# Second feed-forward of a two-block transformer: up products with the weight tile stationary and 256 token columns moving, in place of token tiles stationary, 512 weight columns moving and transposes

## The reference

```python
def squared_relu_mlp(h, w_up, w_down):
    return jnp.square(jax.nn.relu(h @ w_up)) @ w_down

# second block: D_MODEL = 2048, D_FF_2 = 8192
hm = modulate(rms_norm(x, norm_mlp_w[layer]), sh_m, sc_m)
x = x + g_m * squared_relu_mlp(hm, w_mlp_up[layer], w_mlp_down[layer])
return rms_norm(x, final_norm_w)
```

## Time and profile before

| | |
|---|---|
| device time, median of 3 runs | 2152.56 us (2151.63 to 2153.01) |
| profiled execution, span from first to last instruction | 3618.6 us |
| mean granted TensorE clock in the profiled execution | 0.555 |
| TensorE busy | 3602.4 us, 10171 matmuls |
| weight loads busy | 2135.9 us |
| VectorE busy | 1553.3 us |
| ScalarE busy | 1100.0 us |
| read from memory | 483 MB |

### The profile page before, as it was taken

One profiled execution on the slowest core, in us unless ns is written; L12 is line 12 of the kernel. 1 busy time (PEld: TensorE's weight loads), 2 busy tenths in 40 slices (PEclk: granted clock), 3 DMA queues, 4 the chain that ended last, 5 costly groups with the idle time before them and its releaser, 6 DMA issues.

```text
span 3618.6 us, 32275 instructions
## 1 busy us (share of the span) xinstructions
PE 3602.4 (100%) x10171; PEld 2135.9 (59%) x10171; DVE 1553.3 (43%) x1903; ACT 1100.0 (30%) x1467; POOL 129.4 (4%) x232
## 2 busy tenths in 40 slices
PE   9999999999999999999999999999999999999999
PEld 5556855555555555555555567565555555555555
DVE  5555455554555554444453332343333323333334
ACT  3223423333223332233353242232222222222222
POOL 1000000000000000000000000000000000000000
PEclk5555555555555555555555555555555555555555
DMA  7544064555555555544433311344434434433432
GB/s 232 174 147 140 18 198 141 174 162 164 167 175 163 162 166 164 168 145 150 137 105 112 111 53 48 115 134 136 120 118 133 128 117 134 134 112 127 133 104 66
DMA packets 279981, 487.04 MB, mean 135 GB/s; under 512 B 26252, under 2 KB 118740, under 8 KB 278560
## 3 DMA queue, kind: packets, MB, share of 16 engines
q1 hardware_dynamic: 249472, 371.42, 33.2%
q0 software_dynamic: 30192, 113.72, 10.2%
q10 hardware_dynamic: 176, 0.08, 0.0%
HBM read 483.00 MB, written 2.11 MB: 134 GB/s over the span
## 4 chain that ended last, share of the span: by engine, by line
PE 99%; DMA 0%; ACT 0%; POOL 0%; DVE 0%; issue 0%; ACTq 0%; DVEq 0%; POOLq 0%
PE G L1968 29%; PE G L1967 29%; PE G L1966 29%; PE T L2244 2%; PE T L2396 1%; PE T L2160 1%; PE T L2000 1%; PE G L2376 1%; PE G L2140 1%; PE T L2048 0%; PE G L2033 0%; PE G L2032 0%; PE G L2031 0%; PE T L2185 0%; PE T L2187 0%; PE G L2408 0%
## 5 line engine op out<-in xcount | busy, mean ns | idle before, releaser
L1122 DVE TENSOR_TENSOR w_lo<-raw,w_hi 128x1024 fp32r<-128x1024 f32 (+1 forms) x704 | 857.9, 1219 | 1725.4 <-ACT w_hi L593 1723.6
L593 ACT ACTIVATE w_hi<-raw 128x1024 fp32r<-128x1024 f32 (+1 forms) x704 | 741.6, 1054 | 2018.6 <-PE G L1968 2007.7
L1966 PE MATMUL G<-w_hi,h_hi 128*128 128x512 f32 (+1 forms) x1656 | 955.7, 577 | 1.5 <-DVE h_lo L1222 1.0
L1968 PE MATMUL G<-w_hi,h_lo 128*128 128x512 f32 (+1 forms) x1656 | 950.4, 574 | 0.0
L1967 PE MATMUL G<-w_lo,h_hi 128*128 128x512 f32 (+1 forms) x1656 | 947.7, 572 | 0.0
L1966 PE MATMUL G<-w_hi,a_hi 128*128 128x512 f32 x1120 | 650.8, 581 | 0.0
L1967 PE MATMUL G<-w_lo,a_hi 128*128 128x512 f32 x1120 | 645.3, 576 | 0.0
L1968 PE MATMUL G<-w_hi,a_lo 128*128 128x512 f32 x1120 | 645.1, 576 | 0.0
L1966 PEld LDWEIGHTS G<-w_hi,h_hi 128*128 128x128 f32 x1656 | 363.9, 220 | 263.6 <-issue 154.2
L1968 PEld LDWEIGHTS G<-w_hi,h_lo 128*128 128x128 f32 x1656 | 361.4, 218 | 267.7 <-issue 155.5
L1967 PEld LDWEIGHTS G<-w_lo,h_hi 128*128 128x128 f32 x1656 | 364.8, 220 | 259.1 <-issue 152.6
(11 more groups left out here) (289 smaller groups left out, 1425.3 us busy)
## 6 DMA issues: line engine op xcount, KB each, us to landing
ada_w<-in_w_ada POOLq DMA_DIRECT2D x192, 512.0 KB, 3.9
raw<-in_w_up SPq DMA_DIRECT2D x352, 256.0 KB, 2.9
raw<-in_w_mlp_up SPq DMA_DIRECT2D x256, 256.0 KB, 2.8
raw<-in_w_mlp_down SPq DMA_DIRECT2D x256, 256.0 KB, 3.1
raw<-in_w_in SPq DMA_DIRECT2D x224, 256.0 KB, 2.9
raw<-in_w_down SPq DMA_DIRECT2D x176, 256.0 KB, 3.2
raw<-in_w_out SPq DMA_DIRECT2D x128, 256.0 KB, 3.2
raw<-in_w_in SPq DMA_DIRECT2D x16, 136.0 KB, 2.6
```

The lines of the kernel that those rows point to most:

```text
L593: act.activation(w_hi[:, s % 4, :, 0:width], raw[:, s % 8, :, 0:width], ACT.Copy).then_inc(hi_ready, 1)
L1122: dve.tensor_tensor(w_lo[:, s % 4, :, 0:width], raw[:, s % 8, :, 0:width], w_hi[:, s % 4, :, 0:width].bitcast(F32), ALU.subtract).then_inc ...
L1966: pe.matmul(out, ah, wh, start=f, stop=False)
L1968: mm = pe.matmul(out, al, wh, start=False, stop=l)
```

## The change

Of the second feed-forward's up chunks, the 128x128 tile of weights becomes the stationary operand and the 256 tokens the moving one (`up_steps`): for each tile three matmuls of 256 columns into the same columns of a bank, 24 matmuls a step. The result then has the hidden index on partitions, and `turn_up` is no longer called. An up chunk fills half of each of the four banks of `G` (even chunks) or `T` (odd ones); down chunks 0 and 1 use `G`, 2 and 3 use `T`. ScalarE's ReLU (two instructions of 512 columns, now from four half banks) moves from the chunk's end into the body of the next one; the square moves to VectorE (from `u_buf`), the rounding into `a_hi` to ScalarE. Before the 27 transposes at the start TensorE waits for `e0` instead of `e0 - 2`, that is for the last output bank of the phase before. The first row sum of the last group comes after 6 steps of its down chunk instead of before them.

```diff
+    def up_set(c):
+        return T if c % 2 else G
+    def down_set(c):
+        return T if c >= 2 else G
...
-        def post2(u, du):
-            def square():
-                act.wait_ge(turned, u + 1 + du)
-                act.wait_ge(a_ready, u + du)
-                act.activation(conv[:], tt(0), ACT.Square).then_inc(up_read, 1)
-            return square, lambda: None
-        def group2(s, u, d, du, begun=False, last=False):
+        e0 = FIRST_EVAC["mlp2"]
+        def post2(s, e, u, c, d, de, du):
+            def relu():
+                act.wait_ge(step_done, s + 8 * c + 8 + d)
+                act.wait_ge(bank_evac, e + 2 * c + de)
+                act.wait_ge(up_read, u + c + du)
+                for part in range(2):
+                    act.activation(u_buf[:, part, :].rearrange("p (t n) -> p t n", n=TOK),
+                                   up_set(c)[:, 2 * part:2 * part + 2, 0:TOK], ACT.Relu).then_inc(bank_evac, 1)
+            def high_part():
+                act.wait_ge(up_read, u + c + 1 + du)
+                act.activation(a_hi[:, 4 * c:4 * c + 4, :], conv[:], ACT.Copy).then_inc(a_first, 1)
+            return relu, high_part
+        def group2(s, e, u, d=0, de=0, du=0, begun=False, last=False):
             for c in range(4):
                 if c == 0 and begun:
                     his(s + 8, 3)
                 else:
-                    body(s + 8 * c, d, post2(u + c - 1, du) if c else None)
-                up_evac(c, s + 8 * c + 8, d, ACT.Relu)
...
-        def post2(u, c, du):
-            def split():
-                dve.wait_ge(up_read, u + 1 + du)
-                dve.tensor_copy(a_hi[:, 4 * c:4 * c + 4, :], conv[:]).then_inc(a_first, 1)
-                dve.wait_ge(a_first, u + 1 + du)
+        def post2(e, u, c, de, du):
+            def square():
+                dve.wait_ge(bank_evac, e + 2 * c + 2 + de)
+                flat = u_buf[:].rearrange("p b (t n) -> p (b t) n", n=TOK)
+                dve.tensor_tensor(conv[:], flat, flat, ALU.mult).then_inc(up_read, 1)
+            def low_part():
+                dve.wait_ge(a_first, u + c + 1 + du)
                 dve.tensor_tensor(a_lo[:, 4 * c:4 * c + 4, :], conv[:], a_hi[:, 4 * c:4 * c + 4, :].bitcast(F32),
                                   ALU.subtract).then_inc(a_ready, 1)
-            return lambda: None, split
-        def group2(s, u, d, du, first=0, dk=0, dt=0, begun=False, last=False):
+            return square, low_part
...
+        def up_steps(s, k0, k1, banks, ready, d=0):
+            for k in range(k0, k1):
+                pe.wait_ge(hi_ready, s + k + 1 + d)
+                pe.wait_ge(lo_ready, s + k + 1 + d)
+                pe.wait_ge(*ready(k))
+                for j in range(STEPK):
+                    kt = STEPK * k + j
+                    for t in range(CK):
+                        wh, wl = (w[:, (s + k) % 4, j, P * t:P * t + P] for w in (w_hi, w_lo))
+                        pe.matmul(banks[:, t, 0:TOK], wh, h_hi[:, kt, :], start=kt == 0, stop=False)
+                        pe.matmul(banks[:, t, 0:TOK], wh, h_lo[:, kt, :], start=False, stop=False)
+                        mm = pe.matmul(banks[:, t, 0:TOK], wl, h_hi[:, kt, :], start=False, stop=kt == KT - 1)
+                mm.then_inc(step_done, 1)
+        def down_steps(s, k0, k1, c, ready, d=0):
+            for k in range(k0, k1):
+                step(s + k, c % 2, A, STEPK * k, k == 0, k == 7, ready(k), d, banks=down_set(c))
...
-        def group2(s, e, u, d=0, de=0, du=0, begun=2, last=False):
+        def group2(s, e, u, d=0, de=0, du=0, begun=0, last=False):
             def ready(k):
                 return a_ready, u + k // 2 + 1 + du
-            if begun == 2:
-                steps(s, 0, 2, 0, H, r, e - 2, d, de)
             for c in range(4):
-                steps(s + 8 * c, 2 if c else begun, 8, c % 2, H, r, d=d)
-                if c < 3:
-                    steps(s + 8 * c + 8, 0, 2, (c + 1) % 2, H, r, e + 2 * c, d, de)
+                if begun == 0 or c:
+                    pe.wait_ge(bank_evac, e + (-4, 0, 2, 4)[c] + de)
+                up_steps(s + 8 * c, 0 if c else begun, 8, up_set(c), r, d)
+            for c in range(4):
+                pe.wait_ge(bank_evac, e + (6, 6, 8, 8)[c] + de)
+                first = s + 32 + 8 * c
+                if last and c == 0:
+                    down_steps(first, 0, 6, c, ready)
+                    pe.wait_ge(bank_evac, e + 8)
+                    row_sum(0)
+                    down_steps(first, 6, 8, c, ready)
+                elif last and c == 1:
+                    down_steps(first, 0, 4, c, ready)
+                    row_sum(1)
+                    down_steps(first, 4, 8, c, ready)
+                elif last and c == 3:
+                    pe.wait_ge(row_added, 2)
+                    down_steps(first, 0, 4, c, ready)
+                    last_steps(first + 4, A[0], 8, ready, 4, down_set(c))
                 else:
-                    steps(s + 32, 0, 2, 0, A, ready, e + 6, d, de)
-                turn_up(u + c, e + 2 * c + 2, d, du, de)
-            for c in range(4):
-                if last and c == 0:
-                    row_sum(0)
-                if last and c == 1:
-                    steps(s + 40, 0, 4, 1, A, ready, e + 8, d, de)
-                    row_sum(1)
-                    steps(s + 40, 4, 8, 1, A, ready, d=d)
-                else:
-                    steps(s + 32 + 8 * c, 2 if c == 0 else 0, 4 if last and c == 3 else 8, c % 2, A, ready, e + 8 + 2 * (c - 1), d, de)
-            if last:
-                last_steps(s + 60, A[0], 8, ready, 4)
-        pe.wait_ge(bank_evac, e0 - 2)
+                    down_steps(first, 0, 8, c, ready, d)
+        pe.wait_ge(bank_evac, e0)
         keep_busy(27, 0)
-        begin("up2", y, s0, 0, r)
+        begin("up2", y, lambda k: up_steps(s0, k, k + 1, up_set(0), r))
         group2(s0, e0, u0, begun=3)
         with pe.Fori(0, GROUPS2 - 2) as g:
             group2(s0 + 64, e0 + 16, u0 + 4, g * 64, g * 16, g * 4)
```

More of the change, by code:

```diff
@@ L1429, in _, with weighed @@
         first_fold(3)
-        def weighed(c, b):
-            dve.tensor_tensor(y[:, b, c * N:c * N + N], G[:, 2 * (c % 2) + b, :], row[:, c * N:c * N + N],
+        def weighed(c, b, banks=G):
+            dve.tensor_tensor(y[:, b, c * N:c * N + N], banks[:, 2 * (c % 2) + b, :], row[:, c * N:c * N + N],
                               ALU.mult).then_inc(bank_evac, 1)
@@ L1923, in g_row @@
             dve.wait_ge(row_added, half + 1)
[L1925 removed]
+        s0, e0, u0 = 2 * FIRST_LOAD["mlp2"], FIRST_EVAC["mlp2"], UP0["mlp2"]
         dve.wait_ge(y_zero, 1)
[L1927 removed]
+        group2(s0, e0, u0, begun=True)
         with dve.Fori(0, GROUPS2 - 2) as g:
[L1929 to L1930 removed]
+            group2(s0 + 64, e0 + 16, u0 + 4, g * 64, g * 16, g * 4, 8, g * 8, g * 4)
+        group2(s0 + 64 * (GROUPS2 - 1), e0 + 16 * (GROUPS2 - 1), u0 + 4 * (GROUPS2 - 1), first=8 * (GROUPS2 - 1), last=True)
         partial_means("final")
@@ L1952, in _, with step @@
     def _(pe):
-        def step(s, parity, acts, kt, first, last, ready=None, d=0, width=N):
+        def step(s, parity, acts, kt, first, last, ready=None, d=0, width=N, banks=G):
             pe.wait_ge(hi_ready, s + 1 + d)
@@ L1962, in step @@
                     for b in range(NB):
-                        out = G[:, 2 * (parity if n == 0 else 1) + b, 0:width]
+                        out = banks[:, 2 * (parity if n == 0 else 1) + b, 0:width]
                         ah, al = hi[:, kt + j, b * P:b * P + P], lo[:, kt + j, b * P:b * P + P]
@@ L2006, in turns, with begin, last_steps @@
                 turn(name, src, q)
-        def begin(name, src, s, parity, ready):
+        def begin(name, src, first_steps):
             turns(name, src, 0, 3)
-            steps(s, 0, 1, parity, H, ready)
+            first_steps(0)
             turns(name, src, 3, 5)
-            steps(s, 1, 2, parity, H, ready)
+            first_steps(1)
             turns(name, src, 5, 7)
-            steps(s, 2, 3, parity, H, ready)
+            first_steps(2)
             turns(name, src, 7, 8)
-        def last_steps(s, acts, kt, ready, n=2):
+        def last_steps(s, acts, kt, ready, n=2, banks=G):
             for b in range(NB):
@@ L2030, in last_steps @@
                         last = k == n - 1 and j == STEPK - 1
-                        pe.matmul(G[:, 2 + b, :], ah, wh, start=False, stop=False)
-                        pe.matmul(G[:, 2 + b, :], ah, wl, start=False, stop=False)
-                        mm = pe.matmul(G[:, 2 + b, :], al, wh, start=False, stop=last)
+                        pe.matmul(banks[:, 2 + b, :], ah, wh, start=False, stop=False)
+                        pe.matmul(banks[:, 2 + b, :], ah, wl, start=False, stop=False)
+                        mm = pe.matmul(banks[:, 2 + b, :], al, wh, start=False, stop=last)
                     if b == 1:
@@ L2267, in _ @@
                 keep_busy(16, 0)
```

(2 more changed lines are left out.)

24 lines of the change are left out of this document (13 added, 11 removed).

## The result

The changed kernel takes 2159.42 us (median of 6 runs, 2157.65 to 2159.92), the kernel before 2151.62 us beside it (2150.59 to 2153.01): a ratio of 1.0034, 95% interval 1.0024 to 1.0044. It is 7.8 us slower. Forecast were 2142.9 us and 0.45% faster, with a range that ended at 2155.

What follows compares the result with a forecast made beforehand. TensorE was taken as the bound: 2152.56 - 13.5 (transposes) + 3.2 (more matmuls) + 0.6 (later start) = 2142.9 us, 0.45% faster. The stated range was 2137 to 2155 us.

Steps and rivals of the forecast that it cites:

- What bounds the kernel: Whole kernel: TensorE, busy 3602.4 of 3618.6 us; in the changed stage at 2.4 GHz VectorE 59%, transfers 0.73.
- The second rival: Changed stage: transfers or the ScalarE-VectorE chain bound it at 2.4 GHz, so transposes were free; about 2152.5 us, chance 0.10.
- The clock of the timed runs: Timed runs taken to be at 2.4 GHz nearly throughout, inferred from two times, though the profiled execution ran at 0.555.
- The transposes: 8 transposes in each of 16 up chunks removed: 24.3 us of the profiled span, 13.5 us at 2.4 GHz.
- The matmuls: Up products: 1536 matmuls of 512 columns become 3072 of 256, costing 3.2 us more, bounds 0 to 36.6 us.
- the forecast's own range: Timed result from 2138.7 us (14.5 saved, no cost per matmul) to 2147 us (twice the 2.1 ns and some).
- The start: Filler transposes before the changed stage wait for the last output bank: 1.0 us later in the profile, 0.6 us at 2.4 GHz.
- The first rival: All 3072 up matmuls: weight load sets a floor, spacing stays at 205.2 ns; timed 2160 us, chance 0.16.
- The third rival: Up matmuls: cost per matmul at the upper clock takes most of the 13.5 us; 2149 to 2152 us, chance 0.04.
- Moved off TensorE's path: VectorE and ScalarE work per up chunk: all at nothing for the time; VectorE's busy time up 8.6 us.

Runs made afterwards that it cites:

- no_transposes: Kernel before without the 128 transposes of the second feed-forward, ScalarE squaring u_buf instead (hidden values laid out wrongly): 2137.59 us, ratio 0.9935.
- split_256: Kernel before with each 512-column up matmul of the second feed-forward split in two of 256, transposes kept: 2172.31 us, ratio 1.0096.
- before_again: Kernel before, unchanged, run again for a trace at the upper clock (0.999 of 2.4 GHz): 2150.6 us, one run.
- split_128: Kernel before with each 512-column up matmul of the second feed-forward split in four of 128: 2494.01 us, one run.
- tokens_192: Changed kernel with 2688 of the 3072 up matmuls streaming 192 of the 256 token columns: 2135.69 us, one run.
- both_parts: Changed kernel with high and low activations streamed in one 512-column matmul per weight tile, low weights in one of 256: 2151.75 us, ratio 0.9999 to the kernel before.
- wide_then_narrow: Changed kernel, both activation parts adjacent and streamed in one matmul, each slice's four 512-column matmuls before its four of 256: 2148.88 us, ratio 0.9987 to kernel before.
- other_bank: Changed kernel with a slice's 12 matmuls reordered so no two running share a bank or weight tile: 2158.93 us, ratio 1.0034 to the kernel before.

## Why the prediction was wrong

1. **What bounds the kernel: right.** TensorE, in both traces; at 2.4 GHz VectorE is at 59% of the stage before (415.52 of 710 us, 59% predicted) and the transfers at 0.65 (0.73). The second rival (another bound) fell with no_transposes.
2. **The clock of the timed runs: right.** Inferred as 2.4 GHz, measured 0.999 of it.
3. **The transposes: right.** 13.5 us predicted, 13.7 by the medians, 15.0 by the turns and 14.8 by the stage.
4. **The matmuls: the step that failed.** "A pair of them 386.5 instead of 384.4 ns: + 2.1 ns x 1536 = + 3.2 us. [...] I don't scale it, as a cost that doesn't depend on columns need not follow the clock." The cost of one more matmul was read from a line through two widths at 0.555 and carried over unchanged to 0.999. There it is 13 ns, not 2.1: 3072 x 0.120 - 1536 x 0.227 = + 20.0 us instead of + 3.2, and split_256, which has this alone, lost 21.1. At the lower clock a 512-column matmul takes 384 ns, just its columns, and the cost doesn't show; I had no row at the upper clock and took the favourable reading. What the cost is made of stays open: bf16 operands or 64-column loads each take off half of it at 256 columns, and at 512 columns smaller loads take off nothing. The range of that term (0 to 36.6 us) held what was measured, and the forecast's own range didn't use it.
5. **The start: right in kind.** + 0.6 predicted, + 0.5 in the traces. (The 3.3 us there count from the filler's start at 2386.28, not from the last product.) Not predicted: the gap of 0.8 us once in the loop, whose size differs from trace to trace.
6. The sum by what was measured: + 20.0 - 13.7 + 0.5 + 0.8 = + 7.6 us; measured + 7.8. By the two traces alone: four turns of + 1.45 us, + 0.5 at the start and + 0.7 at the loop's turn (1.04 for 0.32) are + 7.0 us, and the stage is 7.0 us longer.
7. **The first rival** was right in its direction, its place and even its time (2160 us, for 2159.4), and was given 0.16. Its mechanism as written, a floor that keeps the 272-column spacing, is half right: there is a floor, at 112 ns, but 256 columns stand above it, and what they pay is dearer spacing at every width from 256 to 512. That its 20.3 us came so near the 20.0 is luck: it rests on 16 columns more (6.6 ns), and the runs have 120 - 227/2 = 6.5 ns for another reason. *The third rival*, given 0.04, named what happened, a cost per matmul at the upper clock without a floor (5 ns and more each extra matmul). It was 13 ns for each extra matmul, so the time lies 7 us and more above its 2149 to 2152. The row of the first rival's floor, 16 load-and-matmul pairs of 65 columns in 3.26 us, takes 1.93 us in before_again at 0.999. The median distance of these matmuls is 112 ns there and 201 in the trace at 0.555, so this floor follows the clock (201/112 = 1.79, 0.999/0.555 = 1.80). The Trainium skill's figure for a load ("TensorE: Matmul & The Clock Gate", "LDWEIGHTS (loading the stationary operand)", 107 ns) was in the text with the remark that it left no margin and doesn't depend on the array's clock. split_128 and tokens_192 have the floor at 112 ns, and by the 201 and 112 ns just named it does depend on the clock. The same page's "Back-to-back issue gap" in the Trainium skill gives an isolated warm matmul its columns and 2.5 ns, which for 512, 256 and 128 columns makes 216, 109 and 56 ns. The runs have 227 and 120 ns for the fp32r matmuls, and 109 ns for the 128-column transposes (before_again), each with a load of its own. The measurement decides.
8. **Moved off TensorE's path: right.** No wait of TensorE on ScalarE or VectorE appears in the stage after its start. VectorE's busy time rose by 8.1 us (1534.3 in before_again, 1542.4 after; 8.6 predicted).

## What to carry to other kernels

Halving the width of TensorE's matmuls isn't free because the columns are the same: here it cost 13 ns for each added fp32r matmul at 2.4 GHz, more than the transposes that it saved (8 of 109 ns a chunk against 96 added matmuls). Read such costs at the clock the kernel is timed at: the profile at half clock showed 2 ns of them. To drop transposes, keep the moving side wide, as the version that streams both parts of the activations past one weight tile does, and measure that too: of the 6 us that it was to win over the kernel before, the first form won nothing (both_parts) and the best 3 us (wide_then_narrow), because the wide matmul came out dearer. And compare the stage that was changed, from one fixed place in the trace: here the phases before it moved by up to 3.6 us between runs of the same code, as much as some of the effects looked for.

## What the runs showed of the hardware

- At 0.999 of 2.4 GHz a matmul of fp32r operands with its own 128-column load follows the one before after 227 ns (512 columns), 125 (272), 120 (256), 112 (192 and 128). With 64-column loads and 64 output partitions, or with bf16 operands, 256 columns take 113 ns.
- At 0.555 the same 512 and 272 columns take 384 and 205 ns, 0 and 1 ns above one column a period (384.4 and 204.2).
- Where the load sets the pace it follows the granted clock: f32 pairs of 65 columns with a load of 128 stand 201 ns apart at 0.555 and 112 at 0.999 (medians), as the clocks do (1.80 times).
- Using the same weight tile twice running, or another bank each time, changes nothing at 256 columns (other_bank).
- The profiler's execution of one and the same kernel ran at 0.555 once and at 0.999 another time.
